# Gate weights: low parts by an adding transfer, and two low parts moved

## The chip, the cores and the metric

The kernel runs on one core of one Trainium2 chip. The metric is the device time of an execution in microseconds (us). The kernel before takes 1695.56 us, the median of three runs (1695.36 to 1696.67).

## The reference

`first_block` is two transformer layers on 256 tokens of width 1024, with adaptive layer norm, an attention or convolution mixer, and a mixture of 16 experts with two chosen per token. A second block with two layers follows. Its layer takes the normed input through one wide product, whose last 4096 columns are the gates of four branches:

```
z  = rmsnorm(x) @ w_in                      # 2520 columns for the mixers, 4096 for the gates
o  = [mla(z), nsa(z), fox(z), dsa(z)]       # four attention mixers, 256 columns each
y  = sum(sigmoid(gate[n]) * (o[n] @ w_branch[n]) for n in range(4)) @ w_out
x  = x + y;   x = x + ffn(rmsnorm(x))
```

All is float32, and the kernel keeps nearly that precision on a TensorE that multiplies in a shorter format (`float32r`).

## The kernel before

**Split products.** To keep precision, weights and activations are split into a high part, rounded to `float32r`, and a low part, what is left. A product is then three: high by high, high by low, low by high (`mm3`, lines 224 to 226). A weight chunk goes through three steps: SyncE loads it into a raw slot; ScalarE copies it into a high slot, which rounds it (`a_split`); VectorE or GpSimd subtracts that from the raw chunk (`v_split`, `g_split`). The low part is written over the raw chunk: `lo` and `raw` are the same bytes. Which engine subtracts is fixed per kind of chunk by `source`, here GpSimd for the gates (`"gt"`).

**Order.** Each engine has its own program, written out by hand, and they meet at semaphores alone. SyncE loads the chunks in the order in which TensorE uses them, each as soon as its raw slot is free. ScalarE, VectorE and GpSimd call `a_split`, `v_split` and `g_split` at places of their programs with a key and `ahead`: all chunks that are not yet done, up to `ahead` behind the key, are done there. A chunk's high part waits until its raw data landed and until the last user of its high slot is done.

**Gates.** In each of the two layers of the second block, 32 gate chunks of 128 x 1024 (512 KB) are TensorE's filler work between the steps of the mixers (`t_fill`, `a_fill`, `v_fill`, `g_fill`; the steps are woven by `weave` in `t_mixers` and its counterparts). A gate chunk takes 12 products of 512 columns. There are six half-size raw slots and four half-size high slots for them. Every fourth chunk completes a gate, whose two banks ScalarE empties with a tanh (`big` in the profile). ScalarE, VectorE and GpSimd also have the mixers' own steps in their queues: evictions, rotations, softmax.

**The output projection.** After the gates come the lifts of the four branches, `mixed` sums and their transposes; `v_mix` writes the low parts of the transposed sums (`hTl`). Then comes the product with `w_out`, in chunks `("wo", l, h, i)`. VectorE makes the low part of `("wo", l, 0, 0)` in `v_fill`, and of the others behind `v_mixers`.

**End of layer 0's experts.** TensorE adds the experts' results into four banks, half h = 0 first (`t_scatter`). `v_moe_out` adds these to `x`, ScalarE squares `x` (`a_stats`), VectorE makes the diagonal of the norm's factors from the sums (`v_diag`), and TensorE multiplies by it (`t_norm`). `v_norm` empties the banks. The next weights are the chunks `("ov", 0)` and `("ov", 1)`. ScalarE makes both high parts ahead of `a_stats`; VectorE makes the low part of the first ahead of `v_moe_out`.

Of the kernel before, what the change touches and what calls it, by code (L numbers as in the profile page):

```python
# [17 lines left out]
NR, RFREE, NH = 7, 5, 5  # L18
# [25 lines left out]
SEMS.update({f"free{b}": f"the last reader of bank {b} has emptied it" for b in range(8)})  # L44
SEMS.update({f"raw{r}": f"a chunk of weights landed in slot {r}" for r in range(NR + 2 * RMIX)})
SMALL = ("sil", "cst", "col", "x", "cx", "row", "pos", "gb00", "gb01", "gb10", "gb11", "fg")
SEMS.update({f"in_{k}": f"{k} landed" for k in SMALL})


# [4 lines left out]
class Book:  # L54
# [21 lines left out]
    def chunk(self, key):  # L76
        c = self.chunks[key] = Chunk()
        c.key, c.epoch, c.n = key, self.epoch, len(self.order)
        c.src, c.how = self.source(key)
        c.parts, c.width = c.src.shape  # L80
        c.r, c.before = self.turn_of("Q" if key[0] == "gt" else "R", key)
        c.raw = self.raws[c.r][0:c.parts, 0:c.width]
        self.order.append(c)
        if c.how in ("dve", "pool"):
            h, c.last = self.turn_of("H", key)
            c.s, c.hi, c.lo = len(self.split), self.his[h][:, 0:c.width], self.los[c.r][:, 0:c.width]
            self.split.append(c)
        return c
# [201 lines left out]
def source(t_in, key):  # L290

    name, at = key[0], key[1:]

    def part(w, i, n=PIECE):
        return w[:, n * i:n * i + n]

    if name == "mod":
        l, p, i = at
        return part(t_in["wmod"][l, p], i), "raw"
    if name in ("kv", "q", "p"):  # L300
        return part(t_in["we_" + name], at[0], 1024 if name == "kv" else PIECE), "dve" if name == "q" else "pool"
    if name == "pm":
        return t_in["pm"], "raw"
    if name == "eo":
        return part(t_in["we_out"][at[0]], at[1]), "dve"
    if name == "gu":
        return t_in["wgu"][at[0], 0, at[1] % 4, at[2]], "dve" if at[1] < 12 else "raw"
    if name == "dn":
        return t_in["wdn"][at[0], 0, at[1] % 4], "pool" if at[1] < 12 else "raw"
    if name == "ov":  # L310
        return part(t_in["wo_v"], at[0]), "dve"
    if name in ("u", "hx", "bg", "cg"):
        return t_in["wo_" + name][at[0]], "dve"
    if name == "oo":
        return part(t_in["wo_out"][at[0]], at[1]), "dve"
    if name == "z":
        l, i, s = at
        a = 8 * ZO[i] + 4 * ZW[i] * s
        return t_in["wz"][l, :, a:a + 4 * ZW[i]], "pool" if i % 2 else "dve"
    if name == "gt":  # L320
        return part(t_in["wgt"][at[0], at[1]], at[2], 1024), "pool"
    if name == "cmp":
        return t_in["wcmp"][at[0]], "raw"
    if name == "mla":
        return t_in["wmla"][at[0]], "raw"
    if name == "br":
        return t_in["wbr"][at[0], at[1]], "raw"
    if name == "wo":
        return part(t_in["wout"][at[0], at[1]], at[2]), "dve"
    if name == "up":  # L330
        return t_in["wup"][at[0], 2 * at[1] + at[2]], "pool" if at[1] == 0 else "dve"
    assert name == "dw"
    return part(t_in["wdown"][at[0], at[1]], at[2]), "pool"
# [118 lines left out]
class Net(Tiles):  # L452
# [64 lines left out]
    def a_split(self, a, *key, ahead=3):  # L517
        for c in a.splits(key, ahead):
            a.wait_ge(*a.at("landed", c.key))
            if c.last is not None:  # L520
                a.wait_ge(*a.at(*c.last))
            a.ac(c.hi, c.raw).then_inc(*a.up("hi"))
            a.mark("hi", c.key)

    def v_split(self, v, *key, ahead=3):
# [6 lines left out]
    def g_split(self, g, *key, ahead=3):  # L532
        for c in g.splits(key, ahead):
            if c.how == "pool":
                g.wait_ge(*g.at("hi", c.key))
                g.tt(c.lo, c.raw, c.hi.bitcast(F32), ALU.subtract).then_inc(*g.up("lo_pool"))
                g.mark("lo", c.key)


# [1299 lines left out]
    def v_moe(self, v, l, name, src, extra):  # L1839
        self.v_route(v, l, name)  # L1840
        self.v_low(v, l, 1)
        beside = self.v_second(v, l)
        self.v_gather(v, l, beside)
        self.v_split(v, "gu", l, 0, 0, ahead=1)
        for _ in beside:
            pass
        self.v_mod(v, 1, 10 if l else 3)
        for r in range(15):
            if r < 12:
                self.v_split(v, "gu", l, r, 0, ahead=self.ahead(r))  # L1850
            if r:
                for u in self.tiles_of(r - 1):
                    if r > 12:
                        break
                    w = self.unit(r - 1, u)
                    b = v.bank("hidden", l, w)
                    v.wait_ge(*v.at("hid hi", l, w))
                    v.tt(self.hidT[1][:, w % 4, :, :], self.ps[:, b, 0:256].rearrange("p (f n) -> p f n", f=2),
                         self.hidT[0][:, w % 4, :, :].bitcast(F32), ALU.subtract).then_inc(*v.up(f"free{b}"))
                    v.mark("hid", l, w)  # L1860
                if r - 1 in extra:
                    self.v_mod(v, *extra[r - 1])
            if r < 12:
                self.v_split(v, "gu", l, r, 1, ahead=self.ahead(r))
            if r < 14:
                if r == 0:
                    self.v_weights(v, l)
                for u in self.tiles_of(r):
                    w = self.unit(r, u)
                    b = v.bank("gu", l, w)  # L1870
                    c0 = 304 + 4 * u + (r % 4 if r < 12 else 2 * r - 24)
                    if w >= 2:
                        v.wait_ge(*v.full("hidden", l, w - 2))
                    v.wait_ge(*v.at("silu", l, w))
                    v.wait_ge(*v.at("slot weights", l))
                    v.stt(self.hid[:, w % 2, :], self.ps[:, b, 256:512], self.rt[:, c0:c0 + 1],
                          self.sl[:, w % 2, :], ALU.mult, ALU.mult).then_inc(*v.up(f"free{b}"))
                    v.mark("weighted", l, w)
            if 0 < r < 12:
                self.v_split(v, "dn", l, r - 1, ahead=self.ahead(r))  # L1880
            if r in (4, 8, 12, 14):
                for u in self.tiles_of(r - 1):
                    self.v_y(v, l, u)
        self.v_split(v, *(("z", 0, 0, 0) if l else ("ov", 0)), ahead=0)
        self.v_moe_out(v, l)

    def v_moe_out(self, v, l):
# [361 lines left out]
    def a_fill(self, a, l):  # L2249
        V = self.views2()  # L2250
        for g in range(8):
            for i in range(4):
                self.a_split(a, "gt", l, g, i, ahead=2)
                if i == 3:
                    if g == 0:
                        a.wait_ge(*a.at("used", ("z", l, 5, 1)))
                        a.wait_ge(*a.at("half rstd", l))
                    for q in range(2):
                        b = a.bank("gate", l, g, q)
                        a.wait_ge(*a.full("gate", l, g, q))  # L2260
                        a.ac(V.sg[:, g // 2, q, 512 * (g % 2):512 * (g % 2) + 512], self.ps[:, b, :], ACT.Tanh,
                             scale=self.half_rstd()[:, q:q + 1]).then_inc(*a.up(f"free{b}"))
                yield
# [23 lines left out]
    def v_fill(self, v, l):  # L2287
        V = self.views2()
        for g in range(8):
            for i in range(4):  # L2290
                self.v_split(v, "gt", l, g, i, ahead=2)
                yield
        for i in range(4):
            while not v.lifts:
# [2 lines left out]
            for h, q in self.QUARTERS:  # L2297
# [9 lines left out]
                if i == 3:  # L2307
                    v.wait_ge(*v.at("summed", l, 2, h, q))
                    v.wait_ge(*v.last)
                    v.tt(g2, g2, V.sg[:, v.before, q, 512 * h:512 * h + 512], ALU.add).then_inc(*v.up("dve"))  # L2310
                    v.mark("mixed", l, h, q)
                    if h == 1:
                        self.v_mix(v, l, q)
                yield
# [10 lines left out]
    def g_fill(self, g, l):  # L2325
        V = self.views2()
        for gg in range(8):
            for i in range(4):
                self.g_split(g, "gt", l, gg, i, ahead=2)
                yield  # L2330
        for i in range(4):
            while not g.lifts:
# [931 lines left out]
    def scalar(self, a):  # L3264
# [20 lines left out]
        self.a_split(a, "eo", 1, 0)  # L3285
        xs = lambda *name: (lambda h, t: a.at("x", *name, h, t))
        self.a_moe(a, 0, "a1", "eo", EXTRA[0])
        self.a_split(a, "ov", 0, ahead=1)
        self.a_stats(a, "b0", self.x, xs("moe", 0), self.s1, 0)
        for p in (6, 7):  # L3290
            self.a_mod(a, 1, p)
        self.a_norm(a, "b0", self.cadj[:, 3, :], self.shift(1, 0), self.hT, H, [("scale", 1, 0)],
# [28 lines left out]
    def vector(self, v):  # L3321
# [34 lines left out]
        self.v_moe(v, 0, "a1", "eo", EXTRA[0])  # L3356
        self.v_cond_scale(v, 1, 0, self.K("n1a", 8, 8))
        self.v_diag(v, "b0", self.s1, 0)
        self.v_norm(v, "b0", self.cadj[:, 3, :], self.shift(1, 0), self.hT, H, [], [("hT used", "a1")])
        self.v_odd(v)  # L3360
        self.v_moe(v, 1, "b1", "oo", EXTRA[1])
        for l in range(2):
# [1 line left out]
                        [("hT used", ("d", 0)) if l else ("hT used", "b1")])  # L3364
            self.v_z(v, l)
            self.v_mixers(v, l)
            for h, i in ((0, 1), (1, 0), (1, 1)):
                self.v_split(v, "wo", l, h, i, ahead=0)
            self.v_out(v, ("wo", l), None)
            self.v_norm(v, ("d", l), self.K("n2b", 8 * l, 8), None, self.hT, H, [], [("pT used", l)])  # L3370
# [202 lines left out]
```

## Time and profile before

| | us |
|---|---|
| median of three runs | 1695.56 |
| the profiled execution, its own time | 1689.58 |
| its span, first to last instruction | 1687.8 |
| TensorE (PE) busy | 1552.3 |
| VectorE (DVE) busy | 821.4 |
| ScalarE (ACT) busy | 739.6 |
| GpSimd (POOL) busy | 596.5 |

The profile is of one execution. PE is TensorE's multiplies, PEld its weight loads, SP is SyncE, which issues the loads. An instruction's row names what it writes and reads: `loh`, `hih` and `rawh` are the low, high and raw half-size slots of the gates, `lo`, `hi` and `raw` the full-size ones. The mean granted clock of TensorE over the span is 0.959 of its full speed. GpSimd's subtractions of the gates are 156.3 us of its busy time.

### The profile page before, as it was taken

The numbers are of one execution on the slowest core, as the hardware profiler recorded it, in microseconds if no ns is written. First come the engines' busy times: TensorE is split into PE (matmuls) and PEld (weight loads), VectorE is DVE, ScalarE is ACT, GpSimd is POOL, SyncE is SP. The second block draws the span as 40 slices with busy tenths as digits, with TensorE's granted clock in tenths as the row PEclk, the third lists the DMA queues.
The fourth block names the chain that finished last, engine by engine and source line by source line (L and its number), as shares of the span: only waits on it lengthen the run. The fifth ranks groups of instructions, "written<-read, shape, count | busy, mean of one in ns | idle before, by whom it ended". The sixth has DMA issues, their size and how long they took to land.

```text
span 1687.8 us, 23289 instructions
## 1 busy us (share of the span) xinstructions
PE 1552.3 (92%) x9590; PEld 1255.9 (74%) x9590; DVE 821.4 (49%) x1470; ACT 739.6 (44%) x1057; POOL 596.5 (35%) x227
## 2 busy tenths in 40 slices
PE   4999989998998999989889889999998898899997
PEld 4867867874997778568667658999886676489996
DVE  2734477323767764153664452522437833635222
ACT  3334366422436654143445344444434454444442
POOL 1200034320000442225555234655546442246543
PEclk7999889999998899999899999999999899999999
DMA  9597269669625686753343344555443333445550
GB/s 386 193 329 270 98 266 344 253 251 373 237 100 200 238 326 234 272 198 122 116 131 124 118 159 165 181 196 171 179 145 118 116 112 126 158 148 205 185 189 26
DMA packets 51225, 327.22 MB, mean 194 GB/s; under 512 B 5936, under 2 KB 5936, under 8 KB 17456
## 3 DMA queue, kind: packets, MB, share of 16 engines
q1 hardware_dynamic: 51120, 325.73, 53.3%
q8 instruction: 76, 1.25, 0.3%
q14 instruction: 29, 0.24, 0.0%
HBM read 324.66 MB, written 1.05 MB: 193 GB/s over the span
## 4 chain that ended last, share of the span: by engine, by line
PE 74%; DVE 17%; ACT 3%; DMA 3%; issue 1%; POOL 1%; DVEq 0%; SPq 0%; ACTq 0%
PE ps L224 19%; PE ps L226 18%; PE ps L225 18%; PE ps L221 14%; DVE lo L232 4%; DMA raw<-in_wmod 2%; DVE pb L2752 1%; ACT hi L229 1%; PE ps L2701 1%; DVE s L240 1%; DVE z L232 1%; ACT pb L229 1%; DMA raw<-in_wo_v 1%; DVE s L232 1%; DVE pb L232 1%
## 5 line engine op out<-in xcount | busy, mean ns | idle before, releaser
L232 POOL TENSOR_TENSOR lo<-raw,hi 128x2048 fp32r<-128x2048 f32 (+2 forms) x76 | 355.1, 4683 | 646.8 <-ACT hi L229 646.8
L229 ACT ACTIVATE hi<-raw 128x2048 fp32r<-128x2048 f32 (+2 forms) x192 | 350.7, 1858 | 55.8 <-POOL big L232 16.9
L232 DVE TENSOR_TENSOR lo<-raw,hi 128x2048 fp32r<-128x2048 f32 (+1 forms) x116 | 291.7, 2532 | 101.1 <-ACT hi L229 100.9
L232 POOL TENSOR_TENSOR loh<-rawh,hih 128x1024 fp32r<-128x1024 f32 x64 | 156.3, 2456 | 137.2 <-ACT hih L229 136.9
L224 PE MATMUL ps<-hTh,hi 128*128 128x256 f32 x640 | 183.2, 286 | 5.4 <-DVE hTl L232 2.9
L225 PE MATMUL ps<-hTl,hi 128*128 128x256 f32 x640 | 182.2, 285 | 0.0
L226 PE MATMUL ps<-hTh,lo 128*128 128x256 f32 x640 | 182.1, 285 | 0.0
L224 PE MATMUL ps<-hi,hTh 128*128 128x512 f32 (+3 forms) x320 | 119.6, 374 | 16.1 <-DVE lo L232 7.5
L224 PEld LDWEIGHTS ps<-hTh,hi 128*128 128x128 f32 x640 | 124.0, 194 | 7.2 <-issue 3.5
L225 PEld LDWEIGHTS ps<-hTl,hi 128*128 128x128 f32 x640 | 124.1, 194 | 0.5
L226 PEld LDWEIGHTS ps<-hTh,lo 128*128 128x128 f32 x640 | 123.9, 194 | 0.0
L224 PE MATMUL ps<-hih,hTh 128*128 128x512 f32 x256 | 110.3, 431 | 8.7 <-ACT big L229 4.8
L224 PE MATMUL ps<-hi,gh 128*128 128x512 f32 x256 | 107.9, 422 | 11.0 <-DVE lo L232 11.0
L225 PE MATMUL ps<-lo,hTh 128*128 128x512 f32 (+3 forms) x320 | 117.3, 367 | 0.0
L226 PE MATMUL ps<-hi,hTl 128*128 128x512 f32 (+3 forms) x320 | 117.1, 366 | 0.0
L232 DVE TENSOR_TENSOR fTl<-s,fTh 128x512 fp32r<-128x512 f32 x32 | 22.2, 692 | 190.7 <-ACT fTh L229 190.7
L225 PE MATMUL ps<-lo,gh 128*128 128x512 f32 x256 | 104.6, 409 | 0.0
L226 PE MATMUL ps<-hi,gl 128*128 128x512 f32 x256 | 104.4, 408 | 0.0
L226 PE MATMUL ps<-hih,hTl 128*128 128x512 f32 x256 | 104.4, 408 | 0.0
L225 PE MATMUL ps<-loh,hTh 128*128 128x512 f32 x256 | 104.3, 408 | 0.0
L229 ACT ACTIVATE s<-ps 128x512 f32<-128x512 f32 (+2 forms) x68 | 31.0, 470 | 159.0 <-PE ps L226 111.1
L224 PE MATMUL ps<-hi,fTh 128*128 128x512 f32 x256 | 99.8, 390 | 0.0
(306 smaller groups left out, 2986.6 us busy)
## 6 DMA issues: line engine op xcount, KB each, us to landing
raw<-in_wgu SPq DMA_DIRECT2D x64, 1024.0 KB, 5.0
raw<-in_wmod SPq DMA_DIRECT2D x48, 1024.0 KB, 6.9
raw<-in_wdn SPq DMA_DIRECT2D x32, 1024.0 KB, 5.7
rawh<-in_wgt SPq DMA_DIRECT2D x64, 512.0 KB, 3.8
raw<-in_wup SPq DMA_DIRECT2D x32, 1024.0 KB, 4.8
raw<-in_wdown SPq DMA_DIRECT2D x32, 1024.0 KB, 5.1
raw<-in_wz SPq DMA_DIRECT2D x12, 1024.0 KB, 4.7
raw<-in_wbr SPq DMA_DIRECT2D x8, 1024.0 KB, 4.8
```

The source lines that it names most:

```text
L221: return self.e.matmul(o, l, r, start=first, stop=last)
L224: self.e.matmul(o, l[0], r[0], start=first, stop=False)
L225: self.e.matmul(o, l[0], r[1], start=False, stop=False)
L226: return self.e.matmul(o, l[1], r[0], start=False, stop=last)
L229: return self.e.activation(o, a, f, **kw)
L232: return self.e.tensor_tensor(o, a, b, op)
L240: return self.e.scalar_tensor_tensor(out=o, in0=a, scalar=s, in1=b, op0=op0, op1=op1)
L2701: m = t.e.transpose(ps[:, b, 128 * h:128 * h + 128], pb[:, n * h + 128 * kt:n * h + 128 * kt + 128], self.C("ident"))
L2752: o = v.e.tensor_tensor_reduce(pb[:, n * h:n * h + n], ps[:, b[h % 2], n * (h // 2):n * (h // 2) + n], mask(i, n), 1.0, -3e38, ALU.add, AL ...
```

## The change

Three things change.

- A gate chunk's low part: ScalarE copies the raw chunk twice, rounded into the high slot and then, with a factor of -1, rounded in place. What stands in the low slot is then the negated high part. GpSimd issues a transfer that adds the weights from memory to it, which leaves the low part. Each half slot has a semaphore for that. The three engines handle gate chunks three ahead instead of two. The scratch for GpSimd's transfer descriptors grows from 256 to 1024 bytes.
- `ov 0`: VectorE's low part moves from ahead of `v_moe_out` to behind `v_diag`; ScalarE's two high parts move behind the squares of half 0 and of half 1.
- `wo 0 1`: VectorE's low part moves from behind the mixers to behind the last `mixed` sum, ahead of the last `v_mix`. It does so in both layers.

```diff
@@ Book.chunk
-        if c.how in ("dve", "pool"):
+        if c.how in ("dve", "pool", "dma"):
@@ source
     if name == "gt":
-        return part(t_in["wgt"][at[0], at[1]], at[2], 1024), "pool"
+        return part(t_in["wgt"][at[0], at[1]], at[2], 1024), "dma"
@@ a_split
-            a.ac(c.hi, c.raw).then_inc(*a.up("hi"))
+            m = a.ac(c.hi, c.raw)
+            if c.how == "dma":
+                m = a.ac(c.lo, c.raw, scale=-1.0)
+            m.then_inc(*a.up("hi"))
@@ g_split
+            elif c.how == "dma":
+                g.wait_ge(*g.at("hi", c.key))
+                g.e.dma_start(c.lo, c.src, accum_op=ALU.add).then_inc(*g.up(f"low{c.r}", 16))
                 g.mark("lo", c.key)
@@ v_moe (end)
-        self.v_split(v, *(("z", 0, 0, 0) if l else ("ov", 0)), ahead=0)
+        if l:
+            self.v_split(v, "z", 0, 0, 0, ahead=0)
         self.v_moe_out(v, l)
@@ a_fill, v_fill, g_fill
-                self.a_split(a, "gt", l, g, i, ahead=2)
+                self.a_split(a, "gt", l, g, i, ahead=3)
@@ v_fill
                     v.mark("mixed", l, h, q)
+                    if (h, q) == (1, 1):
+                        self.v_split(v, "wo", l, 0, 1, ahead=0)
                     if h == 1:
                         self.v_mix(v, l, q)
@@ scalar
-        self.a_split(a, "ov", 0, ahead=1)
-        self.a_stats(a, "b0", self.x, xs("moe", 0), self.s1, 0)
+        self.a_stats(a, "b0", self.x, xs("moe", 0), self.s1, 0, halves=(0,))
+        self.a_split(a, "ov", 0, ahead=0)
+        self.a_stats(a, "b0", self.x, xs("moe", 0), self.s1, 0, halves=(1,))
+        self.a_split(a, "ov", 1, ahead=0)
@@ vector
         self.v_diag(v, "b0", self.s1, 0)
+        self.v_split(v, "ov", 0, ahead=0)
@@ vector
-            for h, i in ((0, 1), (1, 0), (1, 1)):
+            for h, i in ((1, 0), (1, 1)):
                 self.v_split(v, "wo", l, h, i, ahead=0)
@@ kernel
-        nc = bacc.Bacc(..., dynamic_dma_scratch_size=256)
+        nc = bacc.Bacc(..., dynamic_dma_scratch_size=1024)
```

## Rows read from the trace of the kernel before

**Rows 1.** The page: busy us (share of the span) xinstructions of each engine.
```profile
PE 1552.3 (92%) x9590; PEld 1255.9 (74%) x9590; DVE 821.4 (49%) x1470; ACT 739.6 (44%) x1057; POOL 596.5 (35%) x227
```

**Rows 2.** TensorE's waits, 790 to 950 us: total us, times, longest.
```profile
PE ps L2822 <- DVE z L236: 3.5, 1, 3.5
...
PE ps L2937 <- DVE s L252: 2.3, 1, 2.3
PE ps L224 <- ACT big L229: 2.2, 1, 2.2
PE ps L224 <- POOL loh L232: 2.0, 2, 1.1
PE ps L2476 <- DVE z L232: 2.0, 1, 2.0
```

**Rows 3.** Stretch 790 to 950: busy (x) PE, PEld, DVE, ACT, POOL; clock, DMA, GB/s.
```profile
790.00:950.00 160.00, 142.43 (x779) 110.84 (x778) 86.45 (x265) 78.65 (x161) 83.13 (x46) 0.95 0.38 129
```

**Rows 4.** Timelines of PE, DVE, ACT, 398 to 422: start, us, instruction, [idle before <-releaser].
```profile
398.17 0.50 PE L221 MATMUL ps<-gh,ohT 128*128 128x512 f32 x1
...
407.54 3.70 PE L221 MATMUL ps<-raw,sil 128*32 128x128 f32 x128
419.06 5.69 PE L221 MATMUL ps<-s,x 128*128 128x128 f32 x32 [7.82 <-DVE s L236]
...
407.18 2.29 DVE L232 TENSOR_TENSOR lo<-raw,hi 128x2048 fp32r<-128x2048 f32 x1 [7.57 <-ACT hi L229]
...
414.87 0.69 DVE L232 TENSOR_TENSOR x<-x,s 128x512 f32<-128x512 f32 x1
...
421.17 0.99 DVE L237 TENSOR_SCALAR hT<-ps,cadj,mcol 128x256 f32<-128x256 f32 x2 [2.17 <-PE ps L221]
...
415.59 0.63 ACT L229 ACTIVATE s<-x 128x512 f32<-128x512 f32 x1 [0.80 <-DVE x L232]
```

**Rows 5.** Timelines of DVE and PE around `wo 0 1` of layer 0.
```profile
1000.05 1.29 DVE L232 TENSOR_TENSOR hTl<-ps,hTh 128x512 fp32r<-128x512 f32 x2 [5.08 <-ACT hTh L229]
1001.25 6.68 DVE L232 TENSOR_TENSOR lo<-raw,hi 128x2048 fp32r<-128x2048 f32 x3
...
1003.59 0.80 PE L224 MATMUL ps<-hi,hTh 128*128 128x512 f32 x1 [3.77 <-DVE lo L232]
```

**Rows 6.** The gates' half slots, whole span: duration ns min/median/max; landing in us.
```profile
L232 POOL TENSOR_TENSOR loh<-rawh,hih x64: 2337/2392/3489, 792.3 to 1406.7; 128x1024 fp32r<-128x1024 f32 x64
...
L229 ACT ACTIVATE hih<-rawh x64: 1039/1051/1124, 791.1 to 1405.6; 128x1024 fp32r<-128x1024 f32 x64
...
DMA to landing us min/median/max: 3.6/3.8/7.0
```

**Rows 7.** Timelines of ACT and PE: high parts of chunks 0, 1, 22, products of 0, 23.
```profile
791.15 2.00 ACT L229 ACTIVATE hih<-rawh 128x1024 fp32r<-128x1024 f32 x2
...
898.71 1.05 ACT L229 ACTIVATE hih<-rawh 128x1024 fp32r<-128x1024 f32 x1
...
796.12 0.40 PE L224 MATMUL ps<-hih,hTh 128*128 128x512 f32 x1
...
905.91 0.48 PE L224 MATMUL ps<-hih,hTh 128*128 128x512 f32 x1
```

**Rows 8.** The page, DMA issues: KB each, median us to landing.
```profile
raw<-in_wgu SPq DMA_DIRECT2D x64, 1024.0 KB, 5.0
```

**Rows 9.** Timelines of DVE and POOL: VectorE with and without GpSimd's subtraction.
```profile
797.70 5.16 DVE L232 TENSOR_TENSOR z<-z,col 128x96 f32<-128x96 f32 x4
802.88 0.76 DVE L232 TENSOR_TENSOR z<-z,rt 128x96 f32<-128x96 f32 x4
...
878.39 0.16 DVE L232 TENSOR_TENSOR st<-st,lf 128x4 f32<-128x4 f32 x1
...
900.04 2.19 DVE L232 TENSOR_TENSOR st<-st,lf 128x4 f32<-128x4 f32 x1
...
899.83 2.38 POOL L232 TENSOR_TENSOR loh<-rawh,hih 128x1024 fp32r<-128x1024 f32 x1 [11.01 <-ACT hih L229]
```

More of the change, by code:

```diff
@@ L46 @@
 SMALL = ("sil", "cst", "col", "x", "cx", "row", "pos", "gb00", "gb01", "gb10", "gb11", "fg")
+SEMS.update({f"low{r}": f"a chunk's low part is summed in half slot {r}" for r in range(NR, NR + 2 * RMIX)})
 SEMS.update({f"in_{k}": f"{k} landed" for k in SMALL})
@@ L536, in g_split @@
                 g.tt(c.lo, c.raw, c.hi.bitcast(F32), ALU.subtract).then_inc(*g.up("lo_pool"))
+                g.mark("lo", c.key)
+            elif c.how == "dma":
+                g.wait_ge(*g.at("hi", c.key))
+                g.e.dma_start(c.lo, c.src, accum_op=ALU.add).then_inc(*g.up(f"low{c.r}", 16))
                 g.mark("lo", c.key)
@@ L2290, in v_fill @@
             for i in range(4):
-                self.v_split(v, "gt", l, g, i, ahead=2)
+                self.v_split(v, "gt", l, g, i, ahead=3)
                 yield
@@ L2328, in g_fill @@
             for i in range(4):
-                self.g_split(g, "gt", l, gg, i, ahead=2)
+                self.g_split(g, "gt", l, gg, i, ahead=3)
                 yield
@@ L3564 @@
     for _ in range(2):
-        nc = bacc.Bacc("TRN2", target_bir_lowering=False, num_devices=1, dynamic_dma_scratch_size=256)
+        nc = bacc.Bacc("TRN2", target_bir_lowering=False, num_devices=1, dynamic_dma_scratch_size=1024)
         t_in = {k: nc.dram_tensor(f"in_{k}", v.shape, mybir.dt.from_np(v.dtype), kind="ExternalInput").ap()
```

## The prediction

> **What bounds the kernel now.** I read the page's busy times first: TensorE works for 92% of the span, and no other engine passes 49% [rows 1]. So only TensorE's idle time (1687.8 - 1552.3 = 135.5 us in all) and the time at its lower clock can be won. Next come TensorE's waits in the stretch where the 32 gate chunks of layer 0 are woven into the mixers, 790 to 950 us: 17.6 us of idle time, of which rows 2 show the five entries that the change touches, three of them ended by VectorE. ScalarE is busy for 78.65 of the 160 us there, VectorE for 86.45, GpSimd for 83.13, and the DMA engines for 38% [rows 3]. The stretch of layer 1, from 1260 us, repeats it. Then the timelines around the two moved steps. At the end of layer 0's experts TensorE stands 7.82 us for VectorE's `diag` [rows 4]; before each second half of the output projection it stands 3.77 us for one low part [rows 5].
>
> **Reordering 1, the chunk `ov 0` (once).** VectorE is free after 399.6 us (407.18 - 7.57), but its next instruction is the low part of `ov 0`. That waits 7.57 us for ScalarE's high part, whose weights land late, and the eight residual additions of the experts are queued behind it until 415.56 [rows 4]. After the change these are not behind it. The 40 scatter products run from 398.17 to 407.54 [rows 4], half 0 in the first 20. So its two banks are full at about 402.8. The additions go in four pairs, (415.56 - 409.47) / 4 = 1.52 us each; two pairs end at 405.8. Half 1 is full at 407.2 to 407.6; its pairs end at 410.1 instead of 415.56. From the start of ScalarE's last square to TensorE's norm it is 419.06 - 415.59 = 3.5 us now [rows 4], and stays so: the norm starts at 410.1 + 3.5 = 413.6, 5.5 us earlier. ScalarE's high part of `ov 0` (1.9 us) falls between the squares of the halves, where 406.5 to 408.6 is free. Its low part (2.29 us) now stands on VectorE between `diag` and the norm's evictions, which start at 413.6 + 2.29 = 415.9 instead of 421.17 [rows 4]; the bank they wait for, 421.17 - 419.06 = 2.1 us behind the norm's start, is full at 415.7. That gives 5.3 us. `ov 1` was after the norm already and moves with it. Behind it the wo_u, hx and bg loads are issued as slots come free, so they move as well. I take -5.3 us; the least is -4 (the loads come late), the most -7 (the lower clock after the shorter idle time goes too).
>
> **Reordering 2, the chunk `wo 0 1` (twice).** VectorE is idle for 5.08 us before the last two `hTl`; then it does three low parts, and TensorE starts 2.2 us behind the first of them [rows 5]. The change puts this one into the idle time: its high part was written before it. Then `hTl` ends at 1001.3 and releases TensorE, which now starts at 1003.59. That is -2.2 us. The next low part is bound by its high part (ScalarE, from 1001.4 on, 1.9 us) and is ready at 1005.5; the 24 products of `wo 0 1` last until about 1007, so it is not late. The first product here takes 0.80 us, that of the scatter, of the same shape, 0.50 at the higher clock [rows 4, 5], and five more are slowed; some 1.4 us of that may go with the idle time. I take -2.8 us each (-2.0 to -3.6), -5.6 in all.
>
> **The gates, per layer.** The change removes 32 GpSimd subtractions of 2.39 us and adds 32 ScalarE copies. I price the copies like the high part beside them, 1.05 us [rows 6]. It also adds 32 adding transfers of 512 KB that GpSimd issues. TensorE's own work does not change.
>
> (a) The new way from high part to usable low part. GpSimd's issue has no row here; it lies between 0.3 us (SyncE's issue costs that) and the 2.4 us of the work it replaces. I take 1.2. The landing has none either. Not under the 3.8 us of the plain load of the same bytes [rows 6]; the adding transfer also reads its destination, so I take the 5.0 us of a load of 1024 KB [rows 8]. The upper end is twice the plain landing with some queueing, 8.7. Sum: 2.1 + 1.2 + 5.0 + 0.1 = 8.4 us, 6.2 to 13.3.
>
> (b) What covers it. With `ahead=3` ScalarE makes each high part one filling step earlier, about where it now makes the chunk before it. So the time that is left is from the previous chunk's high part to this chunk's products, but not before TensorE has freed the high slot, four chunks back. Over the layer it is mostly 10 to 17 us; the short ones are these. Chunk 23 has 905.91 - 898.71 = 7.2 us [rows 7], and, read in the same way, chunk 24 has 7.6 and chunk 7 6.9: at 8.4 they are late by 1.2 (24 rides on 23) and 1.5. Against that TensorE's 2.0 us of waiting for GpSimd's `loh` go [rows 2]. Net +0.7. The first two chunks have no step to move to: chunk 0's high part starts at 791.15 and its products at 796.12 [rows 7], 5.0 us, so it is 3.4 us late. 2.0 us of this are idle time now, behind chunk 1, where TensorE waits for VectorE's `z` [rows 2], and `z` comes earlier (d). With some low clock: +2.0.
>
> (c) ScalarE's extra 1.05 us a chunk. It is hidden while ScalarE waits for others, which it does for half of the stretch. It is not from 898.7 to 911.6, where four high parts stand among the evictions, the first at 898.71 [rows 7]: four copies push the last eviction by 4.2 us, less 0.9 of idle time and 1.8 of slack; of the 1.5 left some falls together with (b). One wait of 2.2 us on a gate's eviction (`big`) [rows 2] gets longer by one or two copies. I take +3.0 together, 0 to +7.
>
> (d) VectorE without GpSimd beside it. A 128x4 `st<-st,lf` takes 2.19 us while GpSimd subtracts and 0.16 us alone; four `z<-z,col` take 5.16 us where four of the next kind take 0.76 [rows 9]. I compared each VectorE instruction under a GpSimd subtraction with the fastest of its form: 17 us per layer. Most ends in nothing; on the chains that TensorE waits for are 2.0 us before L2822, 2.0 before L2937 [rows 2], and 1.0 in the smaller ones: -5.0 (the 5.8 at `z` are used in (b)). Between 0 and -9.
>
> Sum per layer: +0.7 + 2.0 + 3.0 - 5.0 = +0.7, so +1.4 for two. The whole: -5.3 - 5.6 + 1.4 = -9.5 us. The profiled execution took 1689.58 us for its span of 1687.8, so it would take 1680.1; the median of the runs is 6.0 us above it, and 1695.6 - 9.5 = 1686.1.
>
> The Trainium skill speaks against this change in two places. "Collectives: The Full Stack", in the section on the bandwidth ceiling, says that an add during a DMA needs two source reads and so halves the rate (1.93 measured there); by it the gate transfers would weigh almost two plain loads each. "SBUF — State Buffer", summary for kernel authors, says that a GpSimd-issued transfer's descriptors are starved while VectorE is in a two-port mode. No row here shows either. What the first would do is the second rival, priced from rows.
>
> **The rivals.** (1) *The relief of VectorE wins.* Rows 9 speak for it, and that VectorE ends most of TensorE's waits. If (d) is -8, (c) +1 and the landing 4 us, the gates give -5 a layer: 1674. Against it: the same chains pass ScalarE, whose load grows by 34 us a layer. (2) *The other side: the adding transfers pace the gates.* A landing of 8.7 us makes (a) 13.3. Then chunk 0 is 8.3 us late, of which 2.0 are idle now, and chunks 7 and 23 are 6 us late each, 18 in all; less the 2.0 of (b), and with (c) and (d), +14 a layer: 1695.6 - 10.9 + 28 = 1713. A us more in (a) counts at these three places, 3 us a layer, so it decides from about 10 us for (a) on, where the gates lose the 5.5 us a layer that the reorderings gain. For it: plain loads take 38% of the DMA engines here at 129 GB/s [rows 3]; the gates are 105 of these, so a second pass at the plain price brings 0.69, at twice the price about 1.0. (3) *Gain and loss are equal.* (c) costs 7 a layer as ScalarE's queue delays the score chains: gates +4.7 each, 1694. (4) *The moves don't pay*, as the loads behind `ov` are late and `hTl` rather than the low part holds TensorE: 1692.
>
> **How the numbers follow.** A measurement tells 0.2%, 3.4 us, from no change. The forecast (1680 to 1691) has 0.52, rival 1 0.16, rival 2 0.17, rival 3 0.10, rival 4 0.05. Faster is the forecast, rival 1 and half of 4: 0.70. Same is rival 3 and the other half: 0.13. Slower is rival 2: 0.17. The range takes in rival 1 and of rival 2 what lies below 12 us for (a), 1703: 1672 to 1703.
>
> **What would show it.** Right: TensorE's wait before the norm at about 413 us is near 2.4 us instead of 7.8, the one before `wo 0 1` 1.6 instead of 3.8; short VectorE instructions in the gates have no 2.2 us; GpSimd's busy time falls by 150 us; ScalarE's grows by 67. The landing of the adding transfers settles rival 2: 5 us or 9. The prediction is wrong if TensorE waits for those landings at more than five chunks a layer, or if ScalarE ends the waits that VectorE ends now.

## The result, and the profile after

The changed kernel takes 1706.5 us, the median of seven runs (1697.49 to 1708.24), against 1695.36 us (1693.17 to 1696.67) for the kernel before. The ratio is 1.0061, with a 95% interval of 1.0041 to 1.0080. It is 10 us slower where 9.5 us of gain were forecast, and outside the range. The profiled execution has a span of 1705.2 us, 17.4 more than before; the profiled execution of before was 6 us faster than its median, so the traces show where the time went, and the ratio how much.

The page of the changed kernel: busy times, the DMA queues (packets, MB, share of 16 engines), and issues with their size and median time to landing.

```profile
PE 1559.5 (91%) x9590; PEld 1260.7 (74%) x9590; DVE 761.0 (45%) x1470; ACT 798.4 (47%) x1121; POOL 493.7 (29%) x227
...
q1 hardware_dynamic: 51120, 325.73, 52.7%
q0 software_dynamic: 9216, 33.56, 10.4%
...
rawh<-in_wgt SPq DMA_DIRECT2D x64, 512.0 KB, 6.0
loh<-in_wgt POOLq DMA_DIRECT2D x64, 512.0 KB, 8.6
```

Against [rows 1] VectorE is 60 us less busy, although it does the same work (1470 instructions), and ScalarE 59 us more. GpSimd is 103 us less busy: 156 us of subtractions went, and 56 us of issuing transfers came. The adding transfers (queue q0) land in 8.6 us, counted from the start of GpSimd's issue, and the plain loads of the gates in 6.0 where they took 3.8 [rows 6].

I matched TensorE's instructions of the two traces by name and order, and read how far each stands from where it stood before. That divides the span's 17.4 us by place:

| Stretch of the span before | shift |
|---|---|
| loads of the first 50 us | +1.7 us |
| the `ov 0` move, 411 to 430 us | -5.7 us |
| the rest, to the gates of layer 0 | -1.2 us |
| gates of layer 0 | +15.3 us |
| `wo` move of layer 0 (1000 to 1045 us) | -3.1 us |
| to the gates of layer 1 | +1.6 us |
| gates of layer 1 | +12.0 us |
| `wo` move of layer 1 | -3.2 us |

The loss is in the gates: all else together is a gain of 9.9 us, and of what it loses, the 1.6 us ahead of layer 1's gates stand in the trace of the moves alone (e1, below) too. First the two moves, in timelines of TensorE and VectorE of the changed kernel (start, us, instruction, [idle before <- releaser]):

```profile
415.34 3.84 PE L222 MATMUL ps<-s,x 128*128 128x128 f32 x32 [2.39 <-DVE s L237]
...
415.20 2.29 DVE L233 TENSOR_TENSOR lo<-raw,hi 128x2048 fp32r<-128x2048 f32 x1
...
1011.00 0.47 PE L225 MATMUL ps<-hi,hTh 128*128 128x512 f32 x1 [1.07 <-DVE hTl L233]
...
1005.03 2.28 DVE L233 TENSOR_TENSOR lo<-raw,hi 128x2048 fp32r<-128x2048 f32 x1
1010.16 1.29 DVE L233 TENSOR_TENSOR hTl<-ps,hTh 128x512 fp32r<-128x512 f32 x2 [2.85 <-ACT hTh L230]
```

TensorE's wait before the norm is 2.39 us instead of 7.82, and its 32 products take 3.84 us instead of 5.69, at the higher clock [rows 4]. Before `wo 0 1` it waits 1.07 us for `hTl` instead of 3.77 for the low part, which now stands in VectorE's idle time [rows 5].

Then the gates: the stretch from 790 to 950 us (columns as in [rows 3]), TensorE's waits from 780 to 980 us, and what the trace has on the tile `loh`.

```profile
790.00:950.00 160.00, 131.02 (x700) 100.52 (x699) 54.20 (x245) 98.92 (x170) 32.14 (x45) 0.93 0.91 223
```

```profile
PE ps L225 <- DMA loh<-in_wgt: 17.9, 7, 5.1
PE ps L225 <- ACT big L230: 4.5, 3, 2.0
PE ps L222 <- POOL pb L233: 3.4, 1, 3.4
...
PE ps L2948 <- DVE s L253: 1.1, 1, 1.1
```

```profile
L230 ACT ACTIVATE loh<-rawh x64: 1037/1046/1071, 786.9 to 1422.2; 128x1024 fp32r<-128x1024 f32 x64
L544 POOL DMA_DIRECT2D loh<-in_wgt x64: 856/875/1537, 788.3 to 1423.6; - x64
...
  POOL pb L233: 15.0, 2
...
DMA to landing us min/median/max: 6.2/8.6/12.4
```

The waits of [rows 2] that VectorE ended have nearly gone: neither `z` has an entry any more, and `s` (then L2937, now L2948) is 1.1 us. In their place are 17.9 us for the adding transfers, at 7 of 32 chunks. The DMA engines are busy for 91% of the stretch instead of 38%. The wait for `pb` is new, too: GpSimd's mixer step stands in its queue behind the issue for a gate chunk, which waits for ScalarE's `loh`, and TensorE waits 3.4 us for it. How the first chunk loses, in timelines of PE, ACT and POOL:

```profile
796.22 0.79 PE L225 MATMUL ps<-hih,hTh 128*128 128x512 f32 x1 [5.11 <-DMA loh<-in_wgt]
...
785.99 1.05 ACT L230 ACTIVATE hih<-rawh 128x1024 fp32r<-128x1024 f32 x1
786.94 1.05 ACT L230 ACTIVATE loh<-rawh 128x1024 fp32r<-128x1024 f32 x1
...
788.31 1.01 POOL L544 DMA_DIRECT2D loh<-in_wgt  x1 [9.77 <-ACT loh L230]
```

From the high part to the products it is 10.2 us, where 5.0 were covered [rows 7]. Over all 64 chunks, from the start of ScalarE's high part to the landing of the sum, it is 11.2 us at the median, 8.7 at the least and 17.5 at the most.

### The profile page after: what moved, and what is told of

Its sections match the earlier page's. It is cut to its first block, busy times and chain, and to the rows that moved or that the text cites. A ratio compares the mean times of both kernels' runs of the same rounds, so it can differ in the third digit from the quotient of the medians.

```text
span 1705.2 us, 23353 instructions
## 1 busy us (share of the span) xinstructions
PE 1559.5 (91%) x9590; PEld 1260.7 (74%) x9590; DVE 761.0 (45%) x1470; ACT 798.4 (47%) x1121; POOL 493.7 (29%) x227
## 3 DMA queue, kind: packets, MB, share of 16 engines
q1 hardware_dynamic: 51120, 325.73, 52.7%
q0 software_dynamic: 9216, 33.56, 10.4%
## 4 chain that ended last, share of the span: by engine, by line
PE 71%; DVE 12%; DMA 8%; ACT 5%; issue 3%; POOL 2%; DVEq 0%; SPq 0%; ACTq 0%; POOLq 0%
PE ps L225 18%; PE ps L226 18%; PE ps L227 18%; PE ps L222 15%; DMA loh<-in_wgt 6%; DVE lo L233 4%; DMA raw<-in_wmod 2%; ACT pb L230 1%; DVE pb L2763 1%; ACT loh L230 1%; ACT hi L230 1%; ACT hih L230 1%; PE ps L2712 1%; POOL lo L233 1%; DVE pb L233 1%
## 5 line engine op out<-in xcount | busy, mean ns | idle before, releaser
L544 POOL DMA_DIRECT2D loh<-in_wgt x64 | 56.1, 897 | 245.2 <-ACT loh L230 238.5
```

Source lines behind the costliest of these rows:

```text
L544: g.e.dma_start(c.lo, c.src, accum_op=ALU.add).then_inc(*g.up(f"low{c.r}", 16))
```

## The experiments

Ratios are to the kernel before, run in turns on the same chip, with 95% intervals. A hundredth is 17 us, or 8.5 us a layer for what is done in both layers. "The moves" are the `ov 0` and the `wo 0 1` reorderings. The kernels of e3, e4, e7, e10, e12 and e14 leave out or replace work on the gates' low parts, so their products multiply other numbers; no run tests whether the numbers themselves matter to the time.

| Kernel | ratio | interval |
|---|---|---|
| the change | 1.0061 | 1.0041 to 1.0080 |
| e1 the moves alone | 0.9911 | 0.9896 to 0.9925 |
| e2 the gates' change alone | 1.0165 | 1.0141 to 1.0188 |
| e4 moves, no subtraction, two ahead | 0.9637 | 0.9620 to 0.9654 |
| e10 the same, three ahead | 0.9635 | 0.9609 to 0.9661 |
| e3 and ScalarE's second copy | 0.9793 | 0.9776 to 0.9810 |
| e7 and a plain GpSimd transfer | 0.9838 | 0.9808 to 0.9868 |
| e12 the change, adding half the columns | 0.9912 | 0.9890 to 0.9935 |
| e5 moves, GpSimd subtracts, three ahead | 0.9956 | 0.9944 to 0.9969 |
| e13 moves, adding transfer for 7 of 32 | 0.9942 | 0.9923 to 0.9961 |
| e9 moves, subtraction in 4 pieces | 0.9876 | 0.9854 to 0.9897 |
| e11 moves, subtraction in 8 pieces | 0.9976 | 0.9956 to 0.9996 |
| e8 moves, VectorE subtracts | 0.9993 | 0.9977 to 1.0009 |
| e14 moves, GpSimd writes and reads nothing | 0.9704 | 0.9680 to 0.9728 |

**e1, the moves alone.** The kernel before with the hunks on `ov` and `wo` only.

> The kernel before with the two moved low parts (ov 0 and wo 0 1) alone; the gates are as before. In the trace of the changed kernel TensorE's instructions stand 5.7 us earlier against before over the ov move and 3.1 and 3.2 us over the two wo moves. Theory T (all of the loss is in the gates, the moves pay in full): -12 us, 1683.4. Rival (the moves gain only in the company of the gates' change, since the shift is measured where both differ): within 4 us of before.

0.9911: -15 us by the ratio, 2.5 us more or less; by TensorE's place in the trace -5.7 at `ov`, -3.1 and -4.1 at `wo`. The moves pay by themselves, and somewhat more than forecast (-10.9).

**e2, the gates' change alone.** The changed kernel with those hunks undone.

> The kernel before with the gates' change alone; the moves are undone. Theory T: the two gate stretches lose 15.3 and 12.0 us in the trace of the changed kernel, so +27 us against before, 1722. Rival (loss and gain depend on each other, as the gates are late because the stretch begins earlier in the loads' order): under +18 us.

1.0165, +28 us. With e1's -15 it makes +13, against the change's +10 (interval 7 to 14). Within these intervals the two parts add.

**e3, no adding transfer.**

```diff
             m.then_inc(*a.up("hi"))
             a.mark("hi", c.key)
+            if c.how == "dma":
+                a.mark("lo", c.key)
@@ g_split
-            elif c.how == "dma":
-                g.wait_ge(*g.at("hi", c.key))
-                g.e.dma_start(c.lo, c.src, accum_op=ALU.add).then_inc(*g.up(f"low{c.r}", 16))
-                g.mark("lo", c.key)
```

> The changed kernel without the adding transfers: ScalarE's two copies stay, the low slot keeps the negated high part (so the gates' low parts are wrong), and TensorE waits for ScalarE alone. Theory T (the transfers' landing of 8.6 us is the loss): TensorE's 33 us of waits for them go, and VectorE keeps its relief: at or under the moves alone, 1676 to 1683. Rival A (ScalarE's extra copies are the loss, through its queue): still 10 us or more above the moves alone, 1694 and over.

0.9793: 45 us under the change and 20 us under the moves. It came out below the range of theory T, so what goes with the subtraction is worth more than I had thought. What is left of TensorE's waits, first line here, second in e10, where the second copy is gone too (780 to 970 us, layer 0):

```profile
PE ps L225 <- ACT big L230: 9.1, 5, 2.8
```

```profile
PE ps L227 <- ACT big L232: 0.9, 1, 0.9
```

**e4, no subtraction at all.** Both moves; the gates become a kind "act" for which ScalarE makes the high part alone, and `c.lo = c.hi`.

> The kernel before with both moves, and the gates' subtraction left out: TensorE multiplies with the high part where it used the low part. ScalarE makes one copy, GpSimd does nothing for the gates, no added transfer. It shows what GpSimd's subtractions cost at most, by their wait and through VectorE. By the prediction's terms (5.0 us of VectorE's relief, 2.0 us of waits for GpSimd and 2.0 to 3.4 at z, a layer): 18 to 21 us under the moves alone, 1664. If VectorE's slowed instructions end in nothing: 4 us under, 1679.

0.9637: 46 us under the moves, 23 a layer, beyond what the prediction's terms make. TensorE's granted clock in the stretch rose too: 1.00 here, 0.94 with the moves alone. In their list of waits (780 to 970 us) these stood and here do not: `z` before L2825, 3.5 us, `z` before L2479, 2.0, `loh` 2.0. I compared each of VectorE's instructions in the stretch from 780 to 960 us with the fastest of the same instruction in e3, e10 and the change, where GpSimd subtracts nothing for the gates. With the moves 22 are longer by over 0.1 us, 28.8 us in all (layer 1, 1250 to 1430 us: 31.3); here it is 0.5 (layer 1: nothing). The two layers make the 60 us by which VectorE is less busy in the changed kernel.

**e10, e3 with one copy.** e3 without `m = a.ac(c.lo, c.raw, scale=-1.0)`, and `c.lo = c.hi`.

> The changed kernel without adding transfers and without ScalarE's second copy (the products use the high part where they used the low part), three ahead. Against the same without the transfers only (0.9793 of before) it prices the second copy, and against the moves with no subtraction (0.9637 of before, two ahead) it prices the step from two to three ahead. Theory A (the copies are the 26 us between those two): 0.964, 1630. Rival (three ahead is the cost, since ScalarE waits for high slots and the tanh evictions stand behind it, 9.1 us of TensorE waits for big in layer 0): 0.972 or more, 1644.

0.9635. Three ahead cost nothing here beyond the intervals, and the second copy costs 0.0158, 26.8 us, 13.4 a layer. The two lines above show how: ScalarE's tanh evictions (`big`) come late, and the next gate's chunk waits for the bank, 8.2 us more in layer 0. The granted clock of the stretch (780 to 960 us) is 1.00 here and 0.95 with the copy.

**e7, a plain transfer in place of the adding one.** `g.e.dma_start(c.lo, c.src)`.

> The changed kernel with GpSimd's transfer as a plain copy of the weights over the low slot instead of an adding one (the gates' low parts are then the whole weights). Same bytes from memory, same issue, same waits. Theory D (the add doubles the engine time, 5.3 against 2.8 us per MB and engine in the changed kernel's page, and with it the queueing): landing 8.6 falls to 5 to 6, DMA share in the gates from 0.85 to about 0.6, time 15 us or more under the changed kernel, 1686 and less. Rival F (the cost is GpSimd's way of issuing: descriptors and their start): landing stays over 7.5 and the time within 8 us of the changed kernel.

```profile
q0 software_dynamic: 9216, 33.56, 6.5%
```

```profile
L544 POOL DMA_DIRECT2D loh<-in_wgt x64: 527/528/720, 783.7 to 1386.6; - x64
...
DMA to landing us min/median/max: 4.0/5.9/8.0
```

The page's line on the queue, and the tile's. 0.9838 and a landing of 5.9 us: theory D. A transfer that GpSimd issues costs 0.0045 (3.8 us a layer, 3 more or less) over none, and the add 0.0223 more (18.9 us a layer). The same bytes took 10.4% of 1705.2 us with the add and 6.5% of 1669.5 without: 5.3 and 3.2 us of the 16 engines a MB, against 2.8 for all of SyncE's loads (52.7% for 325.73 MB). SyncE's loads outside the gates go in larger packets, though. Of packets of 4096 bytes in the gates' stretches the median is 159 ns for SyncE, 174 ns for GpSimd's plain transfer and 328 ns for the adding one. "Collectives: The Full Stack" of the Trainium skill, on the bandwidth ceiling, has a measured 1.93 between the rates of a copying and an adding collective; the trace agrees, with 328/174 = 1.9 between GpSimd's two kinds of transfer.

**e12, the adding transfer over half the columns.** `c.lo[:, 0:512]` and `c.src[:, 0:512]`.

> The changed kernel with the adding transfer over the first 512 of 1024 columns alone (the other half of each low part is left wrong). ScalarE's copies, the issue and the waits are the same; half the bytes. Theory D (the bytes, counted twice because of the add, are the cost): landing falls from 8.6 to 5 or 6, near the plain transfer of all bytes, which took 5.9, and the time to near its 0.984 of before. Rival L (an adding transfer has a long fixed time, whatever its bytes): landing 7.5 and more, time over 0.995.

```profile
q0 software_dynamic: 9216, 16.78, 6.0%
```

```profile
DMA to landing us min/median/max: 4.1/5.9/8.5
```

Half the bytes with the add land as fast as all without it. So the landing goes with the bytes, counted about twice, and a fixed time that makes most of it is excluded. The kernel's time lies between the two expectations: it falls by 25 us, where e7 falls by 38. TensorE's waits for the transfers are 5.3 us here and 3.0 in e7 (layer 0); that explains a part of the difference, the rest is open.

**e9, e11, the subtraction in pieces.** In `g_split` the instruction becomes a loop over 4 (or 8) equal slices of columns.

> Both moves, the gates' subtraction on GpSimd as before but in four pieces of 256 columns, each some 0.7 us. Theory P (what subtractions cost is that VectorE's short instructions are held to the end of a GpSimd instruction, up to 2.2 us each): a held instruction now loses at most about 0.6 us, and 6 to 12 us a layer come back: 10 to 25 us under the moves alone, 0.976 to 0.985 of before. Rival (the cost is the later arrival of the low part, or VectorE loses the same sum in more pieces): within 4 us of the moves alone, 0.989 to 0.993.

> Both moves, the subtraction in eight pieces of 128 columns. In four pieces VectorE's lost time in layer 0 went from 24.5 to 18.5 us only, and the time to 0.9876 of before against 0.9911 for the moves alone. If VectorE gets in between the pieces: 0.982 to 0.986. If it is held again by each following piece, and the pieces' fixed time lengthens GpSimd's work (4 x 0.735 against 2.39 us; 8 x 0.45 expected): 0.988 to 0.993.

```profile
L232 POOL TENSOR_TENSOR loh<-rawh,hih x256: 715/735/1718, 781.4 to 1393.7; 128x256 fp32r<-128x256 f32 x128
```

```profile
L232 POOL TENSOR_TENSOR loh<-rawh,hih x512: 442/459/1440, 781.5 to 1405.1; 128x128 fp32r<-128x128 f32 x171
```

Four pieces (4 x 0.735 = 2.94 us) give 0.9876, the best kernel that computes everything. But it is only 6 us under the moves, the intervals touch, and the two were not run beside each other, so it is not shown to be better than they are. Eight (3.67 us) give 0.9976. The expectation's 24.5 and 18.5 us are sums over the fastest instruction of each form, and come out low where that one was held as well. Compared with the same instruction, as under e4, VectorE loses 28.8 us with the moves, in 22 instructions; with four pieces 21.5 us in 51, with eight 17.9 in 70 (layer 1: 31.3, 20.8 and 21.8 us). More instructions are held, each for less. Meanwhile the low parts come later: TensorE's waits for `loh` are 3.9 us in all with the moves, 10.4 with four pieces and 18.0 with eight.

**e5, three ahead with the subtraction.** `ahead=3` for the gates on all three engines.

> Both moves, GpSimd's subtraction as before, but three chunks ahead instead of two. With no subtraction at all three ahead cost nothing (0.9635 against 0.9637). So the step itself is free, and it may save TensorE's 2.0 us a layer of waits for loh: 0 to 5 us under the moves alone, 0.988 to 0.991 of before. Rival (the subtractions meet other, longer VectorE chains when they come a step earlier): over 0.993.

```profile
PE ps L2825 <- DVE z L236: 5.0, 1, 5.0
PE ps L2576 <- DVE pt L232: 4.4, 1, 4.4
PE ps L2479 <- DVE z L232: 4.1, 1, 4.1
```

0.9956, 7.6 us over the moves: the rival. TensorE waits longer for VectorE's chains (these waits were 3.5, 1.9 and 2.0). The step is free without subtractions (e10) and dear with them.

**e13, seven adding transfers a layer.** In `source`: `how = "dma" if 4 * at[1] + at[2] in (3, 5, 10, 16, 17, 18, 22) else "pool"`.

> Both moves, three ahead, and the adding transfer for 7 of the 32 chunks a layer alone (3, 5, 10, 16, 17, 18, 22): those whose subtraction stood on VectorE's instructions for 2 us each in the trace of the moves, and that have 11 us and more from high part to products. GpSimd subtracts the others. Theory P: 14 of the 23 us a layer that VectorE is held go; the seven copies cost ScalarE 7/32 of 13.4 = 3 us; the seven transfers land in 6 to 7 us, covered. Gain up to 10 a layer if all held time counts, half of it likely: 0.977 to 0.986 of before. Rival (subtractions move a little and hold other instructions instead): as the moves alone, 0.989 to 0.993.

0.9942: 2 us under e5, which is its base with `ahead=3` (within the intervals), and 5 over the moves. Neither expectation: the base was wrong, as I had not priced three ahead beside subtractions. VectorE's lost time falls from 31.3 us in e5 to 20.3 (layer 0), with next to no gain. TensorE's list of waits (780 to 970 us) has in return what e5's has not: 2.7 us for `pb` and 1.5 for a landing, and 4.0 for `big` where e5 has 2.2.

The transfers still land in 8.9 us at the median and 7.1 at the least, though the DMA engines are busy for 50% here (780 to 960 us) and 85% in the changed kernel. Their slow landing is thus their own, and not the crowding. By medians, the first packet starts 3.1 us after the issue's start, the packets span 4.3 us, and the sum has landed 1.3 us behind the last of them; e7's plain ones have 2.4, 2.9 and 0.6. Why the first and the last part are long I did not test.

**e8, VectorE subtracts.** The gates' kind is "dve".

> Both moves, and the gates' subtraction on VectorE instead of GpSimd (1.2 us each by half of the 2.29 us of a full chunk, 37 us a layer). Theory P: VectorE's 17 us a layer of held time go and 37 of own work come, in a queue that ends most waits: within 10 us of the moves alone on either side, 0.985 to 0.997. If the late low part was the cost: faster by 8 us and more, as VectorE takes half of GpSimd's time.

0.9993, 14 us over the moves: just past what theory P allowed. VectorE's own queue is a worse place for the subtraction than GpSimd's.

**e14, GpSimd works but reads nothing.**

```diff
-                g.tt(c.lo, c.raw, c.hi.bitcast(F32), ALU.subtract).then_inc(*g.up("lo_pool"))
+                    g.zero(c.raw).then_inc(*g.up("pool"))
+                    g.wait_ge(*g.last)
+                    g.zero(c.raw).then_inc(*g.up("lo_pool"))
```

> Both moves; for each gate chunk GpSimd writes zeros twice over the raw slot, one after the other, instead of subtracting, and TensorE waits for that and multiplies with the high part where it used the low part. GpSimd reads nothing, and the chunk is still released by GpSimd after its work. Theory H (VectorE is held by GpSimd's reads, and that is the 23 us a layer): as with no subtraction, 0.964 to 0.970 of before. Rival (the later release of the chunk is the cost): 0.980 or more, in proportion to the time the two writes take against 2.39 us.

```profile
L254 POOL MEMSET rawh<- 128x1024 f32 x128 | 121.5, 957 | 139.7 <-ACT hih L231 135.6
```

```profile
847.62 5.82 POOL L254 MEMSET rawh<- 128x1024 f32 x6 [7.00 <-ACT hih L231]
849.64 0.89 DVE L239 TENSOR_SCALAR st<-st 128x4 int32<-128x4 int32 x1
850.75 0.16 DVE L234 TENSOR_TENSOR st<-st 128x4 f32<-128x4 f32 x1
```

```profile
864.33 2.22 DVE L232 TENSOR_TENSOR st<-st 128x4 f32<-128x4 f32 x1
```

The rows are the memsets of three chunks (POOL), and a held and a free instruction of VectorE beside them; the single row is the free one again in e1, where it stands beside a subtraction and is held. 0.9704, at the edge of theory H. GpSimd works 1.9 us a chunk, 80% of the subtraction's time, and this costs 0.0067 over no work at all, the subtraction 0.0274. So about three quarters of the subtraction's 23 us a layer, 17.5 us, come with GpSimd's reads; the rest, and a little of these for the shorter work, may be the later release. VectorE loses 8.1 us here instead of 28.8 (layer 1: 6.1 instead of 31.3).

"SBUF — State Buffer" of the Trainium skill, on who interferes with whom, says that a VectorE instruction with two inputs in SBUF contends with a GpSimd instruction that reads SBUF, not with one that only writes it. The trace agrees: 41 instructions of the two-input operations (TENSOR_TENSOR, SCALAR_TENSOR_TENSOR) run beside the zero-writing in layer 0, and none is longer by even 0.1 us, while with the moves 15 of these operations lose 18.4 us. The 8.1 us that are left are 12 TENSOR_SCALAR instructions and one RECIPROCAL queued behind such a one.

## Why the prediction was wrong

The steps of the ratios split the gates' part, here in us a layer beside the prediction's terms. Their sum is by construction the difference between the change and the moves. Each step is worth what it is in this order; no other order was run, and e5 shows that three ahead cost 3.8 us a layer while GpSimd still subtracts.

| Term | predicted | measured | from |
|---|---|---|---|
| GpSimd's subtraction goes: (d), its 2.0 us of waits, z in (b) | -9 | -23.2 | e4 - e1 |
| three ahead | 0 | 0 | e10 - e4 |
| (c) second copy | +3.0 | +13.4 | e3 - e10 |
| (a), (b) transfer, if plain | | +3.8 | e7 - e3 |
| (a), (b) its add | | +18.9 | the change - e7 |
| (a), (b) together | +6.7 | +22.7 | |
| sum | +0.7 | +12.9 | |

The trace has +15.3 and +12.0.

**The moves** were right in mechanism and place. Norm: 5.4 us earlier for 5.5 forecast, the wait 2.39 for 2.4; the term was -5.3, the trace has -5.7. `wo`: -2.8 each, measured -3.1 and -3.2 (e1: -3.1 and -4.1), with a wait of 1.07 us for the 1.6 forecast. The granted clock over the norm's products is 1.00 instead of 0.65.

**(a), the landing, is the step that failed and turned the sign.** I took 5.0 us from a plain load of 1024 KB, since the adding transfer also reads its destination. It was 8.6, close to the upper end. With the landing part at its forecast (+6.7) the other measured terms would have given -3 us a layer; it was +22.7. I also added an issue of 1.2 us that a landing, counted from the issue's start, already holds; the issue was 0.9, and 0.4 us pass before it. So the way is 2.1 + 0.4 + 8.6 + 0.1 = 11.2 us, as the trace has it. Rival 2 was said to decide from about 10, and it did.

What was missing from the 5.0 is the adding transfer's own time, and not the crowding: 328 ns for a packet that takes 159 as a plain load, and a landing of 8.9 us even beside DMA engines half idle (e13). I had a double price and a DMA share of 1.0 worked out, and put them into the rival alone. The share was 0.91, and it slowed the plain loads from 3.8 to 6.0 us at the median. The slowest adding transfer took 12.4 us, where the slowest of e13's few took 10.2. Of the second warning that the prediction took from the Trainium skill, of starved descriptors, nothing shows here: GpSimd's issue takes 0.875 us at the median whether a TENSOR_SCALAR runs on VectorE beside it (12 of 64) or not, and the four issues over 1 us stand beside an idle VectorE.

**(b)** named 3 places, the trace has waits at 7 chunks in layer 0 and 14 in all, more than the five that were to show the prediction wrong. The first chunk is 5.1 us late for the 3.4 forecast. At my 3 us a layer for each us of (a), 11.2 us would cost 8 more than forecast, and it cost 16. The waits are also worth more than their length: 17.9 and 15.0 us a layer, where e3, without the transfers, gains 22.7.

**(c)** was mis-sized, 3.0 for 13.4. I looked for ScalarE's busiest run and priced its one overflow. But the copies stand ahead of tanh evictions all along, and TensorE waits for a bank five times instead of once (9.1 us against 0.9), with the lower clock behind it (0.95 against 1.00). Being idle half of the time did not hide them.

**(d)** was mis-sized the other way, -5 (-9 with what (b) took) for -23. I had 17 us of VectorE's lost time a layer and wrote that "most ends in nothing". The reading was low: it is 29 and 31 us, as the fastest instruction of a form was often held as well. And about three quarters of it counted: VectorE ends most of TensorE's waits in the stretch, and with the waits the low clock went, too (0.94 to 1.00 from e1 to e4). The signs named for it came: no short VectorE instruction of the changed kernel's gates takes 2.2 us.

The errors of (c), +10, and (d), -14 us a layer, partly cancel, and that is luck. With a transfer that lands in 5.9 us (e7) the kernel is 12 us under the moves and 27 under before: faster, as forecast, but about 1668, past the 1686 of the forecast and even the lower bound of 1672.

Two sums of the prediction do not come out. The upper bound is called 1703 for 12 us of (a); its own 3 us a layer for each us gives 1705 to 1708, and the measured 1706.5 would lie inside. That would have been luck, as the errors of (b), (c) and (d) only happen to add up so. And rival 1's terms, with (b) at a landing of 4 us, give -7 us a layer and 1670, not -5 and 1674.

The chances put 0.17 on the mechanism that came, and priced it at 1713 us for a landing of 8.7; measured were 1706.5 for 8.6.

## What to carry to other kernels

A sum that an adding transfer makes is not free bandwidth: count its bytes about twice against the DMA engines, add this to what they already do in the stretch, and do not take its landing from a plain load: 512 KB took 8.6 to 8.9 us adding, 3.8 as a plain load, whether the DMA engines were 85% or 50% busy. An engine idle for half the time can still charge a large part of an added instruction if it serves a chain in order. And a long GpSimd instruction that reads beside VectorE's short ones can be charged to TensorE where VectorE ends its waits: here 23 us a layer for 32 subtractions, 17.5 of them with the reads, as much as the adding of the transfers (18.9).

## What was not expected of the hardware

The time that VectorE loses does not fall in proportion when GpSimd's instruction is cut: 28.8 us whole, 21.5 in four pieces, 17.9 in eight, with 22, 51 and 70 instructions held (layer 0; in layer 1 eight pieces lose as much as four, 21.8 against 20.8 us). GpSimd's issue of a transfer takes 0.53 us plain and 0.88 us adding, and the same 0.87 for half the bytes. An adding packet of 4096 bytes occupies its DMA engine for 328 ns, a plain one of GpSimd's for 174 and one of SyncE's for 159. TENSOR_SCALAR instructions, of one tensor input, are held even where GpSimd only writes: 12 of them for 7.3 us in e14, where none of 41 of the two-input operations was.
